# Where VectorE's weight splits stand inside a step of the differential attention

## The reference

```
q, k, v, gate = split(rms_norm(x) @ w_in)          # 8 heads, two maps of 64 per head, values of 128
for s0 in (0, 128):                                # blocks of 128 queries, e = s0 + 128 keys
    s   = einsum(q[s0:e], k[:e]) * scale           # two score maps per head
    p   = chunk_causal_softmax(s)
    wts = p[map 0] - lam * p[map 1]
    out = einsum(wts, v[:e])
x = x + (rms_norm(out) * (1 - lambda_init) * silu(gate)) @ w_out
```

## Time and profile before

| | us |
|---|---|
| median of 3 executions | 2056.31 (2056.3 to 2057.76) |
| the profiled execution | 2062.28 |
| its span (first to last instruction) | 2060.5 |
| PE busy | 1963.9 (95%) |
| DVE busy | 1565.9 (76%) |
| ACT busy | 1242.4 (60%) |
| attention of layer a0, in the span | about 99 to 161 |
| attention of layer a1, in the span | about 518 to 590 |

### The profile page before, as it was taken

How to read it: one execution, slowest core, us unless ns; L and a number is a source line. 1 busy time by engine, 2 the same in 40 slices (tenths; PEclk the granted TensorE clock), 3 DMA queues, 4 the chain that set the end, 5 groups by cost and what they waited for, 6 DMA issues and landing times.

```text
span 2060.5 us, 26494 instructions
## 1 busy us (share of the span) xinstructions
PE 1963.9 (95%) x9460; PEld 1639.4 (80%) x9460; DVE 1565.9 (76%) x1871; ACT 1242.4 (60%) x1461; POOL 152.8 (7%) x220
## 2 busy tenths in 40 slices
PE   7989988899989899999999999999999999999998
PEld 6767877777778688888878878888888888888886
DVE  7665966767657554446878898988988888898986
ACT  5462145655654444344867767777777777777775
POOL 4013401322011000000000000000000000000000
PEclk9999999999989999999999999999999999999999
DMA  8422233334324265553459889898998989899894
GB/s 336 143 82 95 94 129 138 123 106 176 108 81 164 82 206 189 194 187 123 172 198 374 344 334 375 330 375 341 363 375 334 371 333 375 344 361 374 328 376 171
DMA packets 70518, 499.99 MB, mean 243 GB/s; under 512 B 8736, under 2 KB 8736, under 8 KB 10528
## 3 DMA queue, kind: packets, MB, share of 16 engines
q1 hardware_dynamic: 70432, 498.87, 64.3%
HBM read 497.79 MB, written 1.05 MB: 242 GB/s over the span
## 4 chain that ended last, share of the span: by engine, by line
PE 83%; DVE 8%; ACT 5%; issue 2%; POOL 1%; DMA 0%; DVEq 0%; SPq 0%; ACTq 0%; POOLq 0%
PE psum L1009 24%; PE psum L1011 23%; PE psum L1010 23%; PE psum L1942 4%; DVE low L976 3%; ACT high L973 2%; PE psum L3373 2%; PE psum L3434 1%; PE psum L1950 1%; ACT h L1678 1%; POOL small L1336 0%; PE psum L1574 0%; PE psum L1958 0%; DVE small L1722 0%; PE psum L1130 0%
## 5 line engine op out<-in xcount | busy, mean ns | idle before, releaser
L976 DVE TENSOR_TENSOR low<-raw,high 128x2048 fp32r<-128x2048 f32 x459 | 1044.6, 2280 | 276.2 <-ACT high L973 275.1
L973 ACT ACTIVATE high<-raw 128x2048 fp32r<-128x2048 f32 x459 | 875.8, 1912 | 384.2 <-PE psum L1011 365.7
L1009 PE MATMUL psum<-high,yT_high 128*128 128x512 f32 (+1 forms) x1672 | 663.8, 397 | 23.6 <-DVE low L976 8.4
L1011 PE MATMUL psum<-high,yT_low 128*128 128x512 f32 (+1 forms) x1672 | 653.7, 391 | 0.0
L1010 PE MATMUL psum<-low,yT_high 128*128 128x512 f32 (+1 forms) x1672 | 652.4, 390 | 0.0
L1009 PEld LDWEIGHTS psum<-high,yT_high 128*128 128x128 f32 x1672 | 315.6, 189 | 95.2 <-issue 21.3
L1011 PEld LDWEIGHTS psum<-high,yT_low 128*128 128x128 f32 x1672 | 315.4, 189 | 67.0
L1010 PEld LDWEIGHTS psum<-low,yT_high 128*128 128x128 f32 x1672 | 316.1, 189 | 60.9
L1009 PE MATMUL psum<-high,hT_high 128*128 128x512 f32 (+2 forms) x560 | 221.2, 395 | 10.3 <-DVE h L1854 6.3
L1011 PE MATMUL psum<-high,hT_low 128*128 128x512 f32 (+2 forms) x560 | 217.4, 388 | 0.0
L1010 PE MATMUL psum<-low,hT_high 128*128 128x512 f32 (+2 forms) x560 | 217.1, 388 | 0.0
(11 more groups left out here) (357 smaller groups left out, 1750.7 us busy)
## 6 DMA issues: line engine op xcount, KB each, us to landing
raw<-in_moe_weights SPq DMA_DIRECT2D x336, 1024.0 KB, 4.8
raw<-in_weights SPq DMA_DIRECT2D x132, 1024.0 KB, 4.9
raw<-in_weights SPq DMA_DIRECT2D x2, 896.0 KB, 4.6
raw<-in_weights SPq DMA_DIRECT2D x2, 768.0 KB, 8.1
x<-in_x SPq DMA_DIRECT2D x2, 512.0 KB, 4.1
raw<-in_weights SPq DMA_DIRECT2D x2, 512.0 KB, 3.5
out_x<-x SPq DMA_DIRECT2D x1, 1024.0 KB, 6.0
const<-in_constants SPq DMA_DIRECT2D x1, 512.0 KB, 8.3
```

The source lines that it names most:

```text
L973: eng.activation(high, raw, ACT.Copy).then_inc(k.high_ready, 1)
L976: eng.tensor_tensor(low, raw, high.bitcast(F32), ALU.subtract).then_inc(k.low_ready, 1)
L1009: pe.matmul(out, lhs.high, rhs.high, start=start, stop=False)
L1011: return pe.matmul(out, lhs.low, rhs.high, start=False, stop=stop)
```

## The change

In `a_attention_vector` the call that issues DVE's splits of step s moves from the end of the step to the place right behind the maximum and the bias of item s. No instruction is added or removed. Nothing changes for ACT, PE, GpSimd and the DMA queue.

```
             v.scalar_tensor_tensor(low, top, -1.0, q_root(k, t, head, 0, 2), ALU.mult, ALU.mult).then_inc(k.lowest_ready, 1)
+        if s >= 1:
+            ahead(k, v, k.banks.ticks[(layer, s - 1)])
         i = s - 1
         if 0 <= i < ITEMS:
...
-        if s >= 1:
-            ahead(k, v, k.banks.ticks[(layer, s - 1)])
         if s == 16:
             add_to_x(k, v, (layer, "out", 0), 0, 0)
```

## The result

| us | before | changed |
|---|---|---|
| median (lowest to highest), 20 executions each | 2057.97 (2054.43 to 2061.89) | 2061.47 (2058.14 to 2064.91) |
| ratio of the medians, 95% interval | | 1.0018 [1.001, 1.0025] |
| the profiled execution | 2062.28 | 2061.93 |
| its span | 2060.5 | 2060.1 |

The changed kernel is 3.5 us slower. The two profiled executions alone would say 0.4 us faster. Where these two statements meet is most of what follows.

The account below looks back on a forecast made before the run. The prediction took the order of DVE's work, in a ring with PE and ACT, as the bound inside the two attentions. +1.7 us in a0 and +1.65 in a1 made +3.3 on 2056.3: 2059.6 us, range 2055.5 to 2063.

Parts of the forecast that it names:

- the price as lost cover: Each moved split costs the part of W and `y` that now lies in ACT's high half of the same granule.
- 0.76, 0.34 and 0.54: Slips in us of the next item's maximum and bias on DVE, at steps 3, 9 and 11 of a0.
- W: An item's three DVE instructions of combined weights, taken as 0.76 us at 128 keys and 0.88 at 256.
- Step 2: Granule 15's split: nothing lost on DVE in a0, PE about 0.8 us late; 0 to 0.1 in a1.
- rival 2: New PE idle stretch at step 10 drops the clock as well: +4.7 to +6.7 us, 2061 to 2063; chance 0.16.
- Step 9: Granule 17's split: +0.34 us on DVE; PE gets its weights 1.75 us late, which does not set what follows.
- rival 1: PE's clock stays up where it fell: only +0.5 to +1.9 us, 2056.8 to 2058.2; chance 0.2.
- Step 11: Granule 18's split behind ACT's high half, then combined weights, then `y`: next maximum at about 136.7, +0.54 us.
- M(12): Maximum and bias of item 12 on DVE, forecast about 0.9 us later against step 9.
- Rival 4: Faster: split fills DVE's wait for POOL in step 11; up to 2.2 us a layer, 2052 to 2054; chance 0.04.
- Rival 3: Hidden, or the exchange as good as none: PE's late pieces absorb the slips; 0, at 2056.3; chance 0.1.
- The signs of being wrong: Biases earlier, PE's wait at step 13 gone, or a layer's attention not 1 to 2 us longer at equal clock.

Follow-up runs that it names:

- the halves: Only the splits of steps 2 and 3, or only 9 and 11, moved, TensorE's idle stretches filled with constant transposes: 2058.22 and 2058.05 us against 2059.97 for before.
- the filled before: Kernel before with 14 constant transposes on TensorE ahead of item 11's transposes in both layers: 2056.61 us against 2058.81, ratio 0.9987.
- filled changed kernel: Changed kernel with constant transposes on TensorE, 16 at item 1 of a0, 12 at items 8 and 10 of both layers: 2059.57 us, ratio 1.0000 to before.
- other orders: Against before: splits one step later, ratio 1.0018; granules 16 and 17 ahead of `y` in steps 7 and 11, 18 at the end of step 14, 0.9998.
- both unfilled halves: Only steps 2 and 3, or only 9 and 11, moved, without added transposes: 2063.51 and 2060.78 us against 2058.81 for before, ratios 1.002 and 1.0014.
- the second filling: Kernel before with 14 constant transposes at item 11 of both layers and 9 more at item 1 of a0: 2057.77 us against 2058.53, ratio 0.9997.

## Why the prediction came out as it did, point by point

- **What moves, and the price as lost cover: right.** Only the four splits a layer moved. The terms 0.76, 0.34 and 0.54 measured 0.71, 0.35 and 0.52; the sum of 3.3 us measured 3.29 at equal clock, and the halves add. Lengthening W changed the distances where the lost cover says it must and nowhere else. That a1's step 2 costs nothing and its step 3 in full also holds.
- **On the median.** 3.3 us were laid on 2056.3, the median of three executions. With twenty, before is at 2057.97, 1.7 us higher, and the difference is 3.5. Of the 1.9 us between 2059.6 and 2061.47 the level makes 1.7 and the change 0.2. Three executions are few for a kernel whose executions spread over 7 us.
- **Step 2, TensorE "late by about 0.8 us": right as a delay, wrong as a harmless one.** DVE lost nothing there, as said. But TensorE's idle time of 1.20 us at 106.45 was joined with the delay into one of 2.22 us in front of 107.31, and the clock fell in a0. The half of the change with only steps 2 and 3 shows what that can cost. The new fall was priced in rival 2, but its place was named as step 10 alone. In a0 the place was step 2. Unfilled and filled, this half's attention takes 52.43 and 49.79 us in a0, so the fall cost 2.6 in that execution.
- **Step 9, 1.75 us late at PE, not setting what follows: right for the order.** Measured idle 1.63 in a0, with the clock up behind it, and 1.75 in a1, with a fall from 561.4.
- **The clock, taken at zero: right in the sum, not for the reason given.** I took zero as the idle time as a whole hardly changes. What happened is that rival 1's gain and rival 2's loss came together. With the idle stretches filled, a1's attention takes 48.29 us before and 49.91 changed; unfilled it takes 49.90 and 49.88. So before's fall at 568.3 cost it 1.6 us, near the 1.4 of the prediction, and the changed kernel's fall at 561.4 cost nothing. That hid the order's 1.6 us. In a0 before's fall at 138 cost 1.5 us, and the two of the changed kernel, at 107 and 138, cost 1.8. How this balances over many executions isn't seen in two profiles. The medians differ by 3.5 us with the clock in play. The filled kernels' means differ by 2.8 (1.6 to 3.9), though the filled before of that pair still had a fall in a0, and by 1.8 (give or take 1.9) with the one that had none. All three hold the order's 3.3, and none is fine enough to say what share of the change is the clock's, or with which sign.
- **Step 11: right.** The split started at 134.71, right behind the high half, `y` at 137.77 without a wait for POOL, and M(12) 0.87 later against M(9) (0.35 + 0.52). Rival 4 fell for the reason given, the high half's late end, and the experiment with the splits ahead of `y` showed a second reason: a split in that idle time holds GpSimd's operations up.
- **Rival 3, hidden: fell.** It would have shown in the equal-clock distances. I looked for cover in TensorE's pieces and found none. The four prices on DVE make 1.58 and 1.59 us a layer and the attention grows by 1.67 and 1.62 at equal clock, so there is none.
- **The signs of being wrong.** One of the three came: TensorE's wait at step 13 is gone in a0 and down to 0.52 us in a1. The prediction had it come 0.9 us later. What the runs show is that in a0 TensorE stalls one step sooner, 1.77 us at 137.91 for the weights of item 10, and in a1 the half clock from 561.4 takes the idle time up. With the clock kept up, 0.45 us were left in front of item 11 in a0 of the filled changed kernel. The biases did not come earlier, and the layer is longer by the 1 to 2 us asked for, so the price stands; the path by which TensorE meets it was read wrong there.
- **The rule of the two sides of SBUF.** In the changed kernel GpSimd's last operation began at 133.85, before the split at 134.71, took 1.04 us as ever, and the split didn't wait for it, so the zero was right. But my reading of the earlier trace rows went too far. They show that a DVE operation which begins second isn't held, and nothing of a GpSimd operation that begins second. That one is held: 2.15 and 2.19 us in place of 0.24 and 0.20. The Trainium skill, page "SBUF — State Buffer", section "SBUF: two separate sides", says that the two lock each other out for a whole instruction. The runs here agree for GpSimd under a split and do not for DVE under GpSimd's operation.

The two missed expectations of gains of 0.2 to 0.4% from other orders had one fault in common: I judged a place by DVE's idle time alone. One kept TensorE from its weights, the other held GpSimd's operations up. Three more expectations missed in size: both unfilled halves cost more than expected, and the second filling gained less.

## What to carry to other kernels

When an instruction that waits is moved ahead of others on an engine that works in order, ask what used to run during its wait; the price is that overlap, read from the row of the releasing engine, and not the instruction's length. A place for movable work is free only if the engine's next consumer, the engine it waits for and the one behind it in the ring can all do without it. Compare two orders with idle stretches filled, or over many executions, since here one profile of each hid 3.5 us.

## What the runs showed of the chip

- A 2.3 us two-input operation on VectorE over 128x2048 stretched a GpSimd operation over 128x4 from 0.20 to 2.19 us and from 0.24 to 2.15, to its own end. In the other direction 0.48 us on VectorE ran inside 1.03 us on GpSimd.
- TensorE's clock fell to 0.50 behind idle stretches of 1.75, 1.77, 2.22 and 2.40 us in the attentions of the profiled pair and stayed up behind one of 1.63. But in the kernel with only steps 2 and 3 moved it stayed at 1.00 behind 2.39 us in front of 141.25. Behind 1.20 us at 106 it stayed up in before's profile and was low in others that do the same work up to there (from 107.3 in the one with steps 9 and 11 moved, from 106.2 in the filled before). So one profile doesn't say whether an idle stretch of such a length costs clock.
- A fall can cost its attention 1.6 us (a1 of before, at 568.3) or nothing (a1 of the changed kernel, at 561.4), by the same distance with and without filling.
- With nothing changed ahead of it, the first maximum of a0 starts anywhere from 97.8 to 100.4 us in the 14 profiles. So spans of single profiles can differ by 2.6 us before the first changed instruction.
- Kernels with TensorE kept busy spread less: the five filled ones over 2.9 to 5.0 us (11 executions each), the two unfilled halves over 7.0 and 10.3 (11 each), before over 8.7 (33).
